# A hybrid decoder layer on one core: expert sums kept in PSUM, a ring of 24 weight slots, and a finer last transfer

## The chip, the core and the metric

The kernel runs on one core of a Trainium2 chip. The metric is the device time of one execution, in microseconds. TensorE is called PE below, VectorE DVE, ScalarE ACT, GpSimd POOL and SyncE SP. A transfer is a DMA that SP or ACT issues into its own queue.

## The reference, cut to what matters

The input is 256 tokens of 1024 float32 channels. A first part (norm, a combined projection, three mixers, merge gates, an output projection) adds to the residual `h`. A second part is a mixture of 32 experts in 4 groups; each token takes the best group and its two best experts there. The reference computes every expert for every token and weighs the results:

```
xn = rms_norm(h, norm2_g)
for e in range(32):
    hid = silu(xn @ w1[e]) * (xn @ w3[e])          # 1024 -> 256
    out = out + combine[:, e:e + 1] * (hid @ w2[e])  # 256 -> 1024
h = h + out
return rms_norm(h, final_norm_g)
```

The weights of the experts are 96 MiB in float32, and each is read once.

## The kernel before, in words

**The ring.** Nearly all weights pass through `ring`, a buffer of `SLOTS` = 22 slots, each of 2048 floats on 128 partitions (1 MiB). In the first part of the kernel the slots hold that part's weights, their high and low halves and scratch; each slot is given to an expert chunk by `early(...)` (L514) as soon as its last other use is over. Small buffers such as `qT`, `att`, `con`, `hidg` and `hidu` lie beside the ring.

**Expert chunks.** Four experts (`EB`) make a block, there are 8 blocks, and a block has 12 chunks: chunks 0 to 7 are the eight 128-row pieces of `w1` and `w3`, chunks 8 to 11 are `w2` by quarters of 256 output columns. Two rounds of four blocks (`ROUND` = 4) make one pass, and the inputs need one pass. So 96 chunks are loaded: 22 of them early, 74 while the experts are computed.

**Which slot a chunk takes.** `AT` gives the slot of each of the 48 chunks of a round: `[0..21, 0..17, 4..7, 18..21]`. SP issues the chunks in order. Ahead of each it waits until `expert_used` says that the chunk that held the slot (`earlier(c)`) was used: first six single chunks (L582), then pairs of 2 MiB (L585), the round's last two singly (L588), and for the second round the same in a loop (L596, L600). The queue is in order, so a chunk that waits for its slot holds back all behind it. By `AT`, the chunks 40 to 43 of the first round go into slots 4 to 7, which chunks 26 to 29 held, 14 chunks before.

**A block on PE.** For each of the 8 first chunks, four matmuls (one for each expert, on 32 rows of 128x32 stationary data) add into `bank[0]` (L1759). Between them `gather` (L1727) collects the tokens of the block, with the one-hot matrix `sel`, out of `xn2`, the normed and scaled copy of `h`. Banks 2 and 3 take its halves, ACT copies the one (L895) and DVE the other (L1315) to `xgT`. ACT applies Silu (L900), DVE multiplies (L1323), PE turns the result (L1782), ACT copies it (L902). Then come the four column quarters: `second(qt)` (L1794) multiplies by `w2` into bank 4 or 5, ACT copies the quarter to `yN` (L907), and `combine(qt)` (L1804) spreads it to the tokens by `cmbT`, into banks 6 and 7. DVE adds each result to `h` in SBUF (L1329); PE waits for that (`add_done`) before it writes the bank again. In a block `second(qt + 1)` stands before `combine(qt)`, and the last combine stands alone.

**Before and behind the experts.** POOL multiplies `h` by `norm2_g` into `xn2` (L661), ACT scales that by the token's reciprocal root (L883). PE runs `keep_busy` (L1374) while DVE works out the routing. The gain of the final norm, `fing`, is loaded by ACT at the start of the experts. At the end, ACT squares `h` in three parts as they become final (L926), POOL takes the power -0.5 (L683), DVE and ACT scale one token tile each (L1364, L944), and four transfers of 256 KB write the output.

Of the kernel before, what the change touches and what calls it, by code (L numbers as in the profile page):

```python
# [34 lines left out]
NQT = D // QC  # L35
CAP = 32
# [5 lines left out]
SLOTS = 22  # L42
# [66 lines left out]
K_DIST = K_ID + P  # L109
K_CB = K_DIST + 3 * P  # L110
K_CM = K_CB + NT * HEADS * 16
K_IC = K_CM + NT * 16
K_TRI = K_IC + 2 * T
# [7 lines left out]
K_N = K_FOLD2 + RC  # L121

TAKEN = 1024.0


def build(nc, x, params, consts, front, projs, small, wgrp, vecs, routerw, routerb, experts, out):
    with ExitStack() as ctx:
# [10 lines left out]
        def sem(name):  # L138
# [6 lines left out]
        con = sb("con", [P, K_N])  # L145
# [11 lines left out]
        qT = sb("qT", [P, REP, T])  # L157
        kv = sb("kv", [P, 4 * T])
        gts = sb("gts", [P, NT, GATES])
        hidg = sb("hidg", [P, 4, 2 * NCMP])  # L160
        hidu = sb("hidu", [P, 4, 2 * NCMP])
# [5 lines left out]
        att = sb("att", [P, 6 * 3 * P])  # L167
        qcur = sb("qcur", [P, T])
        npass = sb("npass", [P, 1], I32)
# [21 lines left out]
        sPT = att[:, 12 * P:18 * P].rearrange("p (b k) -> p b k", b=2)  # L191
# [12 lines left out]
        osplit = over("osplit", [P, 2, 4, T], "att")  # L204
# [18 lines left out]
        qflat = qT[:].rearrange("p r t -> p (r t)")  # L223
        comb = qflat[:, 320:384].rearrange("p (t e) -> p t e", t=NT)
        mask = qflat[:, 384:448].rearrange("p (t e) -> p t e", t=NT)
        rank = qflat[:, 448:512].rearrange("p (t e) -> p t e", t=NT)

        xn2 = att[:, 0:NT * D].rearrange("p (t d) -> p t d", t=NT)
        fin = xn2
# [9 lines left out]
        lg, gap1, key1, first, left, gap2, key2, second_of, both = [  # L239
            qflat[:, 448 + NT * NE // 2 + 32 + i * NT * RC:448 + NT * NE // 2 + 32 + (i + 1) * NT * RC] if i < 6 else  # L240
            qflat[:, (i - 6) * NT * RC:(i - 5) * NT * RC] for i in range(9)]
# [7 lines left out]

        g2b = con[:, K_DIST:K_DIST + D]  # L250
        fing = con[:, K_DIST:K_DIST + D]

        ident = con[:, K_ID:K_ID + P]
        dist = con[:, K_DIST:K_DIST + 3 * P]
# [4 lines left out]
        cmask = con[:, K_CM:K_CM + NT * 16].rearrange("p (t c) -> p t c", c=16)  # L259
        icnt = con[:, K_IC:K_IC + 2 * T].rearrange("p (a t) -> p a t", a=2)  # L260
        rk8 = con[:, K_RK:K_RK + PER_GROUP]
        fold = con[:, K_FOLD:K_FOLD + 32]
        fold2 = con[:, K_FOLD2:K_N]
# [13 lines left out]
        expert_in = [sem(f"expert_in{i}") for i in range(SLOTS // 2)]  # L277
        last_in = sem("last_in")
# [79 lines left out]
        xn2_done = sem("xn2_done")  # L358
        h2T_full = sem("h2T_full")
        h2T_done = [sem(f"h2T_done{i}") for i in range(2)]  # L360
        gained2 = sem("gained2")
# [19 lines left out]
        gained_most = sem("gained_most")  # L381
# [7 lines left out]
        add_done = sem("add_done")  # L389
# [77 lines left out]
        def second_out(qt, rows):  # L467

            return bank[4 + qt % 2][rows, 0:QC]

        def combined(t):

            return bank[6 + t][:, 0:QC]
# [4 lines left out]
        def _(sp):  # L478
# [42 lines left out]
            sp.dma_start(con[:, P:], consts[:, P:]).then_inc(con_in, 16)  # L521
# [38 lines left out]
            front_chunk(CH_NSA, 1)  # L560
            front_chunk(CH_WO, 0)
# [4 lines left out]
            front_chunk(CH_WO + 1, 1)  # L566

# [10 lines left out]
            early(SLOT_XHI, SLOTS)  # L578

            for c in range(SLOTS, SLOTS + SINGLES):  # L580
                sp.wait_ge(expert_used, earlier(c) + 1)
                sp.dma_start(ring[:, AT[c]], single(c)).then_inc(expert_in[AT[c] // 2] if c % 2 else single_in, 16)  # L582
            for c in range(SLOTS + SINGLES, NC - 2, 2):
                sp.wait_ge(expert_used, earlier(c + 1) + 1)
                sp.dma_start(slots_of(c), experts[c // NQ, c % NQ // 2]).then_inc(expert_in[AT[c] // 2], 16)  # L585
            for c, sem_in in ((NC - 2, expert_in[AT[NC - 2] // 2]), (NC - 1, last_in)):
                sp.wait_ge(expert_used, earlier(c) + 1)
# [1347 lines left out]
```

## Time and profile before

| | |
|---|---|
| median of 3 runs | 422.76 us (422.14 to 422.81) |
| the profiled execution's own time | 422.27 us |
| its span, first to last instruction | 420.4 us |
| outside the span | 1.87 us |
| mean granted PE clock | 0.985 |
| PE, DVE, ACT busy in the span | 388.5, 201.9, 141.7 us |
| bytes moved by transfers | 140.29 MB, mean 334 GB/s |
| first expert matmul | 219.42 us after the span's start |

Times in the rows are from the start of the span. The time beside the span is launch and end work that the trace doesn't show.

### The profile page before, as it was taken

What the parts mean: (1) busy time and instruction counts of PE and PEld (TensorE: products, weight loads), DVE (VectorE), ACT (ScalarE), POOL (GpSimd) and SP (SyncE); (2) the same over time, 40 slices, a digit from 0 to 9 for tenths busy, and PEclk for the clock granted to TensorE, in tenths of its full rate; (3) what the DMA queues carried; (4) which work ended last, traced back from release to release, by engine and by line L of the source; (5) the groups of instructions that cost most, each with busy time, mean ns of one, the idle gap of its engine ahead of it and who ended that gap; (6) DMA issues with size and microseconds to landing.
All of it is one profiled execution on the core that took longest, in us unless ns stands there. A gap on an engine that the chain in (4) does not pass through costs nothing.

```text
span 420.4 us, 7086 instructions
## 1 busy us (share of the span) xinstructions
PE 388.5 (92%) x2802; PEld 259.2 (62%) x2802; DVE 201.9 (48%) x392; ACT 141.7 (34%) x257; POOL 18.9 (4%) x39
## 2 busy tenths in 40 slices
PE   7999999999999999999989999999999778779682
PEld 5998988677777777888764545454435324234241
DVE  3838683999898595683362323231222203103113
ACT  6734352638565535242340303030302003011014
POOL 3000000300000000000520000000000000000002
PEclk9999999999999999999999999999999989979998
DMA  8999999634352495578999999899999999999972
GB/s 308 419 409 341 405 380 372 225 142 143 119 191 74 152 372 175 197 282 330 416 400 331 431 426 426 330 432 424 427 429 426 424 432 426 432 427 427 426 321 100
DMA packets 16871, 140.29 MB, mean 334 GB/s; under 512 B 2128, under 2 KB 2512, under 8 KB 5072
## 3 DMA queue, kind: packets, MB, share of 16 engines
q1 hardware_dynamic: 15696, 138.07, 81.9%
q10 hardware_dynamic: 1152, 1.88, 1.3%
q8 instruction: 17, 0.28, 0.3%
q14 instruction: 6, 0.05, 0.0%
HBM read 138.90 MB, written 1.05 MB: 333 GB/s over the span
## 4 chain that ended last, share of the span: by engine, by line
PE 69%; DMA 21%; DVE 6%; issue 1%; ACT 1%; POOL 0%; SPq 0%; POOLq 0%; DVEq 0%; PEldq 0%
DMA ring<-in_experts 20%; PE bank L1759 10%; PE bank L1794 5%; PE bank L1531 5%; PE bank L1727 5%; PE bank L1804 4%; PE bank L1532 4%; PE bank L1533 4%; PE bank L1389 4%; PE bank L1391 4%; PE bank L1390 4%; PE bank L1652 2%; PE bank L1654 2%; PE bank L1653 2%; PE bank L1493 1%; PE bank L1519 1%
## 5 line engine op out<-in xcount | busy, mean ns | idle before, releaser
L1759 PE MATMUL bank<-ring,kv 128*32 128x512 f32 x512 | 67.6, 632 | 13.4 <-DMA ring<-in_experts 13.3
L461 DVE TENSOR_TENSOR part<-ring,part 128x2048 fp32r<-128x2048 f32 (+1 forms) x26 | 57.8, 2231 | 16.9 <-ACT part L454 16.9
L454 ACT CAST part<-ring 128x2048 fp32r<-128x2048 f32 (+1 forms) x26 | 48.0, 1847 | 30.5 <-DMA ring<-in_front 30.3
L1329 DVE TENSOR_TENSOR h<-h,bank 128x256 f32<-128x256 f32 x64 | 26.9, 421 | 60.2 <-PE bank L1804 59.8
L1727 PEld LDWEIGHTS bank<-qcur,att 128*128 128x128 f32 x256 | 31.7, 191 | 28.2 <-issue 28.2
L1531 PE MATMUL bank<-part,xhi 128*128 128x512 f32 x96 | 39.2, 408 | 0.0
L1727 PE MATMUL bank<-qcur,att 128*128 128x128 f32 x256 | 39.1, 289 | 0.0
L1794 PE MATMUL bank<-ring,hidT 128*32 128x256 f32 x512 | 33.8, 385 | 4.8 <-DMA ring<-in_experts 4.2
L900 ACT ACTIVATE cw<-bank 128x256 f32<-128x256 f32 x8 | 3.1, 383 | 103.8 <-PE bank L1759 103.8
L1532 PE MATMUL bank<-part,xhi 128*128 128x512 f32 x96 | 37.5, 391 | 0.0
L1533 PE MATMUL bank<-part,xlo 128*128 128x512 f32 x96 | 37.5, 391 | 0.0
L1759 PEld LDWEIGHTS bank<-ring,kv 128*32 128x32 f32 x512 | 12.8, 111 | 39.9 <-issue 25.6
L1389 PE MATMUL bank<-xhi,part 128*128 128x256 f32 x128 | 36.6, 286 | 0.5 <-DVE xlo L977 0.5
L1804 PE MATMUL bank<-gab,vbd 128*128 128x256 f32 x128 | 36.2, 405 | 0.7
L1390 PE MATMUL bank<-xlo,part 128*128 128x256 f32 x128 | 36.2, 283 | 0.0
L1391 PE MATMUL bank<-xhi,part 128*128 128x256 f32 x128 | 36.2, 283 | 0.0
L1804 PEld LDWEIGHTS bank<-gab,vbd 128*128 128x128 f32 x128 | 21.0, 188 | 16.1 <-DVE h L1329 9.2
L907 ACT COPY gab<-bank 128x256 f32<-128x256 f32 x32 | 11.9, 371 | 47.4 <-PE bank L1794 47.4
L1323 DVE TENSOR_TENSOR vbd<-cw,bank 128x256 f32<-128x256 f32 x8 | 3.4, 421 | 50.2 <-ACT cw L900 50.2
L1389 PEld LDWEIGHTS bank<-xhi,part 128*128 128x128 f32 x128 | 24.5, 192 | 1.7 <-DVE xlo L977 0.9
L1794 PEld LDWEIGHTS bank<-ring,hidT 128*32 128x32 f32 x512 | 13.8, 109 | 18.2 <-issue 5.3
L1390 PEld LDWEIGHTS bank<-xlo,part 128*128 128x128 f32 x128 | 24.6, 192 | 0.0
(250 smaller groups left out, 548.8 us busy)
## 6 DMA issues: line engine op xcount, KB each, us to landing
ring<-in_experts SPq DMA_DIRECT2D x32, 2048.0 KB, 29.9
ring<-in_experts SPq DMA_DIRECT2D x32, 1024.0 KB, 8.6
ring<-in_front SPq DMA_DIRECT2D x28, 1024.0 KB, 5.9
ring<-in_front SPq DMA_DIRECT2D x4, 512.0 KB, 6.8
ring<-in_projs SPq DMA_DIRECT2D x4, 512.0 KB, 5.1
ring<-in_front SPq DMA_DIRECT2D x2, 560.0 KB, 9.2
h<-in_x SPq DMA_DIRECT2D x2, 512.0 KB, 3.9
con<-in_vecs ACTq DMA_DIRECT2D x2, 512.0 KB, 7.8
```

The lines of the kernel that those rows point to most:

```text
L454: nc.scalar.copy(high(n, half)[:, 0:c].bitcast(F32R), raw(n, half)[:, 0:c]).then_inc(hi_done, 1)
L461: nc.vector.tensor_tensor(low(n, half)[:, 0:c].bitcast(F32R), raw(n, half)[:, 0:c], high(n, half)[:, 0:c], ALU.subtract).then_inc(split_do ...
L1389: mm(dst, whi, ahi, start=start, stop=False)
L1390: mm(dst, whi, alo, start=False, stop=False)
L1391: return mm(dst, wlo, ahi, start=False, stop=stop)
L1531: mm(bank[t][:], XH[:, kk, cols], whi[:, k], start=(kk == 0), stop=False)
L1532: mm(bank[t][:], XH[:, kk, cols], wlo[:, k], start=False, stop=False)
L1533: ins = mm(bank[t][:], XL[:, kk, cols], whi[:, k], start=False, stop=(kk == KT - 1))
L1727: ins = mm(bank[2 + k // 4][:, (k % 4) * P:(k % 4 + 1) * P], xn2[:, t, k * P:(k + 1) * P], flat(sel[:, t]), start=(t == 0), stop=(t == NT ...
L1759: ins = mm(bank[0][CAP * e:CAP * (e + 1)], xgT[:, q, CAP * e:CAP * (e + 1)], expert(j, q, e), start=(q == 0), stop=(q == NQ1 - 1))
L1794: ins = mm(second_out(qt, slice(CAP * e, CAP * (e + 1))), hT[:, ht, CAP * e:CAP * (e + 1)], second_weights(j, qt, ht, e), start=(ht == 0), ...
L1804: mm(combined(t), cmbT[:, t * P:(t + 1) * P], yN[:, qt * QC:(qt + 1) * QC], start=True, stop=True).then_inc(comb_done, 1)
```

## The change

It has six parts. **Ring:** `SLOTS` is 24 and `AT` is `[0..23, 0..23]`, so that each chunk waits for the one 24 before it. The room comes from `att` and `qT` (with the half of `con` that only the first part reads, now `conf`), which move into slots 22 and 23, from the second copy `xn2`, which is no more, and from `hidg` and `hidu`, now laid over `qcur`. SP loads slot 23 early once `pc_done` is set, and slot 22 after the last NSA projection (`y_full`). **Sums:** before the experts, PE copies `h` into banks 4 to 7 by a matmul with the identity, in place of `keep_busy`. Each combine adds into these banks (`start=False`), the DVE adds and `add_done` are gone, and the squares and final scalings read the banks. `second` uses banks 0 and 3, gather bank 2 alone. **Norm:** gather reads `h` itself. `norm2_g` is applied when `xgT` is copied: four ACT activations of 128x128 in place of one copy of 128x512, and a DVE product in place of its copy. The token's reciprocal root is carried to the slots by two matmuls with one column and is the scale of Silu and of the DVE product. POOL's and ACT's passes over `xn2` are gone. **Pieces:** the columns are combined in five pieces, the last quarter as two of 128. In a round's last block the order is 0, 1, combine 0, combine 1, 2, combine 2, 3, 4, combine 3, combine 4. **Transfers:** a round's last chunk is issued as two halves with a semaphore each; `norm2_g`'s broadcast load is gone, and `fing` is loaded by SP behind the last chunk, into a slot that has become free. **Loop:** PE's code for the last round stands behind the loop as a copy of its own.

```
-SLOTS = 22
+SLOTS = 24
-AT = [*range(SLOTS), *range(18), *range(4, 8), *range(18, SLOTS)]
+AT = [*range(SLOTS), *range(SLOTS)]
+PIECES = ((0, 256), (256, 512), (512, 768), (768, 896), (896, 1024))
...
+            sp.wait_ge(scT_full, 1)
+            sp.wait_ge(pc_done, 1)
+            early(SLOT_Q, SLOTS)
             front_chunk(CH_WO, 0)
...
             front_chunk(CH_WO + 1, 1)
+            sp.wait_ge(y_full, 2 * N_G)
+            early(SLOT_ATT, SLOT_Q)
...
-            for c, sem_in in ((NC - 2, expert_in[AT[NC - 2] // 2]), (NC - 1, last_in)):
+            for c, f, sem_in in ((NC - 2, slice(0, ECHUNK), expert_in[AT[NC - 2] // 2]), (NC - 1, slice(0, half), last_half_in),
+                                 (NC - 1, slice(half, ECHUNK), last_in)):
...
+            sp.wait_ge(expert_used, passes * (NC * NB // ROUND) + (GIVEN - NQ + 2))
+            sp.dma_start(fing[:], vecs.to_broadcast([P, D])).then_inc(vec_in, 16)
...
-                    nc.gpsimd.tensor_tensor(xn2[:, t, c], h[:, t, c], g2b[:, c], ALU.mult).then_inc(gained2, 1)
...
-                nc.scalar.copy(flat(xgT[:, 0:4]), bank[2][:]).then_inc(xg0_done, 1)
+                for k in range(4):
+                    ins = nc.scalar.activation(xgT[:, k], bank[2][:, k * P:(k + 1) * P], ACT.Copy, scale=prm[:, PR_G2 + k:PR_G2 + k + 1])
+                ins.then_inc(xg0_done, 1)
...
-                nc.vector.tensor_tensor(hN, sl1, bank[0][:, HID:2 * HID], ALU.mult).then_inc(hn_done, 1)
-                for qt in range(NQT):
-                    for t in range(NT):
-                        dve.wait_ge(comb_done, b * (NT * NQT) + (NT * qt + t + 1))
-                        hv = h[:, t, qt * QC:(qt + 1) * QC]
-                        nc.vector.tensor_tensor(hv, hv, combined(t), ALU.add).then_inc(add_done, 1)
+                nc.vector.scalar_tensor_tensor(hN, bank[0][:, HID:2 * HID], rslot, sl1, ALU.mult, ALU.mult).then_inc(hn_done, 1)
...
             hidden(blocks)
             second_copy(blocks, 0)
             second_copy(blocks, 1)
-            second_copy(blocks, 2)
             last_square(0, 0)
             last_square(0, 1)
+            second_copy(blocks, 2)
+            last_square(1, 0)
+            last_square(1, 1)
             second_copy(blocks, 3)
-            for n in (1, 2):
-                for t in range(NT):
-                    last_square(n, t)
+            second_copy(blocks, 4)
+            last_square(2, 0)
+            last_square(2, 1)
...
-            keep_busy(8, ident, con[:, K_TRI:K_TRI + 2 * P])
+            for t in range(NT):
+                mm(bank[4 + t][:], ident, h[:, t, 0:512], start=True, stop=False)
+            for qt in (2, 3):
+                for t in range(NT):
+                    mm(summed(t, qt), ident, h[:, t, qt * QC:(qt + 1) * QC], start=(t == 0), stop=False)
...
+                            for t in range(NT):
+                                ins = mm(bank[1][:, T:T + 1], flat(sel[:, t]), stat[:, 26 + t:27 + t], start=(t == 0), stop=(t == NT - 1))
...
-                            pe.wait_ge(add_done, b * (NT * NQT) + (NT * qt + t + 4))
-                            mm(combined(t), cmbT[:, t * P:(t + 1) * P], yN[:, qt * QC:(qt + 1) * QC],
-                               start=True, stop=True).then_inc(comb_done, 1)
+                            ins = mm(sum_of_piece(t, p), cmbT[:, t * P:(t + 1) * P], yN[:, columns(p)],
+                                     start=False, stop=last and j == ROUND - 1 and (p == 1 or p in (2, NP - 1) and t == NT - 1))
+                        ins.then_inc(comb_done, 1)
```

## Rows read from the trace of the kernel before

**Rows 1.** The page: costliest groups, busy and mean, then idle before and its releaser.

```profile
L1759 PE MATMUL bank<-ring,kv 128*32 128x512 f32 x512 | 67.6, 632 | 13.4 <-DMA ring<-in_experts 13.3
L1329 DVE TENSOR_TENSOR h<-h,bank 128x256 f32<-128x256 f32 x64 | 26.9, 421 | 60.2 <-PE bank L1804 59.8
```

**Rows 2.** Windows of whole blocks: length, busy by engine, PEclk, DMA share, GB/s.

```profile
219.40:240.40 21.00, 20.88 (x180) 10.29 (x180) 5.98 (x14) 5.26 (x9) 0.00 (x0) 1.00 0.95 371
282.40:305.00 22.60, 21.65 (x181) 10.18 (x180) 5.71 (x14) 4.04 (x9) 0.00 (x0) 1.00 1.01 428
385.40:413.00 27.60, 22.01 (x181) 10.30 (x180) 5.92 (x15) 4.40 (x14) 1.91 (x2) 1.00 0.80 340
```

**Rows 3.** Windows of the expert stage on either side of the gap at 267 us.

```profile
232.00:266.00 34.00, 33.82 (x295) 17.09 (x288) 9.34 (x22) 7.27 (x14) 0.00 (x0) 1.00 1.01 427
272.00:404.00 132.00, 113.42 (x915) 52.84 (x914) 28.85 (x67) 18.90 (x40) 0.00 (x0) 0.96 1.01 427
```

**Rows 4.** The page's DMA issues: count, KB each, us from issue to landing.

```profile
ring<-in_experts SPq DMA_DIRECT2D x32, 2048.0 KB, 29.9
```

**Rows 5.** Line L600, the two last chunks: first and last start, then time to landing.

```profile
L600 SPq DMA_DIRECT2D ring<-in_experts x2: 333/548/764, 369.5 to 370.1; - x2
...
DMA to landing us min/median/max: 37.5/38.5/39.4
```

**Rows 6.** Windows of 1 us inside the gap.

```profile
267.00:268.00 1.00, 1.00 (x13) 0.36 (x16) 0.80 (x3) 0.00 (x0) 0.00 (x0) 1.00 0.31 131
268.00:269.00 1.00, 1.00 (x14) 0.26 (x8) 0.38 (x1) 0.00 (x0) 0.00 (x0) 1.00 0.12 49
269.00:270.00 1.00, 1.00 (x16) 0.29 (x12) 0.00 (x0) 0.00 (x0) 0.00 (x0) 1.00 1.49 279
270.00:271.00 1.00, 1.00 (x16) 0.23 (x8) 0.00 (x0) 0.00 (x0) 0.00 (x0) 1.00 0.73 295
```

**Rows 7.** Timeline of SP's queue: start, length, line, count.

```profile
184.16 0.33 SPq L495 DMA_DIRECT2D ring<-in_front  x1
...
189.86 1.28 SPq L514 DMA_DIRECT2D ring<-in_experts  x3
...
220.54 7.58 SPq L582 DMA_DIRECT2D ring<-in_experts  x6
...
268.07 2.53 SPq L585 DMA_DIRECT2D ring<-in_experts  x3
```

**Rows 8.** Windows where the two new early loads would fall.

```profile
159.00:162.00 3.00, 3.00 (x17) 2.52 (x16) 0.67 (x1) 2.29 (x2) 0.00 (x0) 1.00 0.69 208
...
189.00:192.00 3.00, 3.00 (x19) 2.58 (x18) 1.11 (x1) 2.83 (x3) 0.00 (x0) 1.00 0.37 76
```

**Rows 9.** Timeline of PE in a block: one second product, one combine.

```profile
252.37 1.07 PE L1794 MATMUL bank<-ring,hidT 128*32 128x256 f32 x16
...
255.01 1.13 PE L1804 MATMUL bank<-gab,vbd 128*128 128x256 f32 x4
```

**Rows 10.** Timeline of the end: PE's last products, ACT's squares.

```profile
404.70 1.93 PE L1794 MATMUL bank<-ring,hidT 128*32 128x256 f32 x32 [0.85 <-DMA ring<-in_experts]
...
409.82 0.63 ACT L926 ACTIVATE kv<-h 128x512 f32<-128x512 f32 x1 [0.68 <-DVE h L1329]
...
410.69 2.34 PE L1804 MATMUL bank<-gab,vbd 128*128 128x256 f32 x8
...
413.10 0.42 ACT L926 ACTIVATE otmp<-h 128x256 f32<-128x256 f32 x1 [0.27 <-DVE h L1329]
```

**Rows 11.** ACT: a plain first copy (timeline), an activation with a scale column (by form).

```profile
218.53 0.37 ACT L910 COPY kv<-bank 128x256 f32<-128x256 f32 x1 [2.62 <-PE bank L1736]
...
L712 ACT ACTIVATE xhi<-bank,prm 128x256 fp32r<-128x256 f32 x8 | 3.3, 492 | 0.1
```

**Rows 12.** Windows and timeline of PE behind long waits for chunks.

```profile
336.00:339.00 3.00, 2.95 (x16) 0.69 (x16) 0.00 (x0) 0.00 (x0) 0.00 (x0) 0.50 0.98 415
...
370.28 3.40 PE L1759 MATMUL bank<-ring,kv 128*32 128x512 f32 x16 [2.10 <-DMA ring<-in_experts]
```

More of the change, by code:

```diff
@@ L221, in build @@
         mlo = over("mlo", [P, KT, T], "ring", SLOT_XLO * SLOT)
[L223 to L229, printed above, removed]
+        routed = over("routed", [P, 3, NT, NE], "wg")
+        comb, mask, rank = routed[:, 0], routed[:, 1], routed[:, 2]
+        fin = over("fin", [P, NT, D], "ring", 12 * SLOT)
+        fing = over("fing", [P, D], "ring", 13 * SLOT)
+        last_squares = over("last_squares", [P, NT, D], "ring", 14 * SLOT)
         xgT = kv[:].rearrange("p (k s) -> p k s", k=KT)
@@ L237, in build @@
         lgT = qcur[:]
-        lg, gap1, key1, first, left, gap2, key2, second_of, both = [
-            qflat[:, 448 + NT * NE // 2 + 32 + i * NT * RC:448 + NT * NE // 2 + 32 + (i + 1) * NT * RC] if i < 6 else
-            qflat[:, (i - 6) * NT * RC:(i - 5) * NT * RC] for i in range(9)]
+        lg, gap1, key1, left, gap2, key2 = [kv[:, i * NT * RC:(i + 1) * NT * RC] for i in range(6)]
+        first, second_of, both = [yN[:, i * NT * RC:(i + 1) * NT * RC] for i in range(3)]
         top1, big1, top2, big2, behind, e2, weight, c1, c2, total = [vflat[:, 256 + 16 * i:256 + 16 * i + NT * ROWS] for i in range(10)]
@@ L465, in xT, with columns, second_out, summed @@
             return bank[(0, 1, 2, 3, 6, 7, 5, 5)[k]][:, (k == 7) * T:((k == 7) + 1) * T]
[L467 to L473, printed above, removed]
+        def columns(p):
+            return slice(*PIECES[p])
+        def second_out(p, rows):
+            return bank[(0, 3)[p % 2]][rows, 0:PIECES[p][1] - PIECES[p][0]]
+        def summed(t, qt):
+            c = t * QC if qt > 1 else qt * QC
+            return bank[4 + t if qt < 2 else 4 + qt][:, c:c + QC]
+        def sum_of_piece(t, p):
+            c0, c1 = PIECES[p]
+            return summed(t, c0 // QC)[:, c0 % QC:c0 % QC + c1 - c0]
         block = ctx.enter_context(nc.Block())
@@ L879, in _ @@
             nc.scalar.copy(lgT, bank[0][:, 0:T]).then_inc(lgT_done, 1)
-            act.wait_ge(gained2, 2 * NT)
-            act.wait_ge(rstd_done, NT + 1)
-            for t in range(NT):
-                nc.scalar.activation(xn2[:, t], xn2[:, t], ACT.Copy, scale=stat[:, 26 + t:27 + t]).then_inc(xn2_done, 1)
-            act.wait_ge(xn2_done, NT)
-            act.dma_start(fing, vecs[1:2].to_broadcast([P, D])).then_inc(vec_in, 16)
             act.wait_ge(sub_done, 1)
@@ L914, in _ @@
                 hidden(b + 1)
-                for qt in range(NQT):
-                    second_copy(b + 1, qt)
+                for p in range(NP):
+                    second_copy(b + 1, p)
                 gathered_copy(b + 1)
@@ L1742, in _, with round_of_blocks @@
             passes = pe.value_load(npass[0:1, 0:1], min_val=1, max_val=MAXPASS)
-            with pe.Fori(0, passes * (NB // ROUND)) as bb:
+            def round_of_blocks(bb, last):
                 for j in range(ROUND):
@@ L1809, in _ @@
                         gather(3)
-                    for qt in range(1, NQT):
-                        second(qt)
-                        combine(qt - 1)
-                    combine(NQT - 1)
+                    second(1)
+                    combine(0)
+                    if j < ROUND - 1:
+                        second(2)
+                        combine(1)
+                        second(3)
+                        combine(2)
+                    else:
+                        combine(1)
+                        second(2)
+                        combine(2)
+                        second(3)
+                    second(4)
+                    combine(3)
+                    combine(4)
+            with pe.Fori(0, passes * (NB // ROUND) - 1) as bb:
+                round_of_blocks(bb, False)
+            round_of_blocks(pe.value_load(npass[0:1, 1:2], min_val=1, max_val=MAXPASS * (NB // ROUND) - 1), True)
 def constants():
```

206 lines of the change are left out of this document (107 added, 99 removed).

## Prediction

> **What bounds the kernel now.** I began at the page's costliest groups [rows 1]. PE is busy nearly all the time, but its largest idle time, 13.3 us, stands before the first expert product and waits for expert chunks. The DVE adds into `h` are short, and DVE waits long before them, so DVE bounds nothing. Next, the windows by block [rows 2]: a block lasts 21.0 us while PE sets the pace (22.6 for a round's last block, where no later gather fills the waits), and 27.6 us in the last, with 22.0 busy. Then the windows of the transfers [rows 3]: 427 GB/s from 232 to 266 us and again from 272 to 404. A block's 12 chunks are 12.58 MB, so 29.5 us at that rate. PE needs 21. The expert stage is therefore a race that starts with a full ring and that the transfers lose: their last landing sets the end. The time from issue to landing, 29.9 us for the pairs [rows 4], says the same: SP issues far ahead. The last two chunks, issued at 369.5 and 370.1 us, landed after 37.5 and 39.4 us: 407.0 and 409.5 [rows 5]. So a chunk takes 2.5 us, by the rate 1.0486 MB / 427 GB/s = 2.46 us. The end is 420.4, which is 10.9 us behind the last landing. The sum has three terms: how many chunks are left when the race starts, where the transfers pause, and the 10.9 us.
>
> **Two chunks fewer in the race.** The stream begins when chunk 0 is used: first issue at 220.54 [rows 7]. With 24 slots 72 chunks are left, not 74: 2 x 2.46 = -4.9 us, if the two others find idle transfer time earlier. Slot 23 is issued once `pc_done` is set, near 159 us, where transfers move 208 GB/s, a share of 0.69 [rows 8]; the queue's next member waits for PE's gate products anyway. Slot 22 is issued when the last NSA product is done, the event that releases the front transfer at 184.16; the next issue is at 189.86 [rows 7], and 189 to 192 us moves 76 GB/s [rows 8]. Each needs 2.5 us and has some 5. If neither fitted, the term would be 0: its other bound.
>
> **The pause goes.** The windows from 267 to 271 us move 131, 49, 279 and 295 GB/s [rows 6]: 296 + 378 + 148 + 132 = 954 KB short of 427, or 2.2 us. SP issues again at 268.07 [rows 7]. By `AT`, chunk 40 takes slot 4, which chunk 26 held; it is in block 2, which begins at 219.4 + 2 x 21.0 = 261.4, so its use is near 267. SP's order holds back all behind. After the change chunk 40 waits for chunk 16, used some 20 us earlier. For any chunk the distance is 24, PE needs 1.75 us for a chunk and the transfers 2.46, so once started they wait for no slot: -2.2 us. Bounds: 0, if the pause has another cause, and -2.2. The last half then lands at 409.5 - 4.9 - 2.2 = 402.4.
>
> **The start of the race.** PE's gather, and so block 0, hardly moves. The first copy of 128x256 took 0.37 us at 218.53 and block 0 began at 219.42, 0.5 us later than the copy allowed [rows 11]. Two activations of 128x128 with a scale column replace it. An activation with a scale of 128x256 took 0.49, a plain copy 0.37 [rows 11]; for 128 columns I bound one by 0.25 and 0.4, so the two by 0.5 and 0.8: both inside the 0.37 + 0.5 us there is. The identity products replace `keep_busy` product for product in columns (2 x 512 + 4 x 256 for 8 x 256) in the wait for DVE's routing; hidden. One more small DVE step lies beside the gather. I take 0. POOL's and ACT's passes over `xn2` were not what PE waited for, so dropping them gains 0. The early broadcast of `fing`, 0.52 MB, leaves a stretch of full transfers: at most -1.2 us, taken as 0 since the next issue waits for chunk 0.
>
> **PE's work per block, and its cover.** Gone: the wait for a DVE add in a lone combine, between nothing and one add (0.42 us [rows 1]); the two last combines take 2.34 us where one takes 1.13 [rows 9, 10], so I take 0.1. Added: two products with one column, bounded by 0 and by the 0.28 us that each of a combine's four records takes, 1.1 us; I take 0.3. ACT's four activations (1.0 to 1.6 us) replace a copy near 0.6 us, between the last piece's copy and the next block: after the last `second`, ACT needs 0.35 + 1.0 to 1.6 us, PE's two half combines 1.1; a wait of 0.3 to 0.9, say 0.6. In a round's last block the combines wait for their copies, some 1 us more. Together +0.7 us a block, 1.0 to 2.0 at the bounds. The cover is PE's lead over the chunks: alone, it would reach the last block's second products at 219.4 + 7 x 21.0 + 1.6 + 14 = 382; the chunks admit it at 404.6 now, 397.5 after. That is 15.5 us for 8 blocks, 1.9 us a block. So this costs 0; beyond 1.9 us each block would pay the excess.
>
> **Behind the last landing.** A second product of 256 columns takes 1.0 us, a combine 1.1 [rows 9]; pieces of 128, half; an ACT copy 0.37, or 0.26 for 128; a pair of squares of 512 columns 1.3 (0.63 each, start to start 0.63 [rows 10]), of 256 0.95, each with its read of the sum. Count from the last landing, X. The pair with quarters 0 and 1 lands at X - 4.9, as now [rows 10]. Second 0 and 1 to X - 2.9, combine 0 and 1 to X - 0.8, second 2 to X + 0.2. ACT now squares ahead of copy 2: to X + 0.6, the copy to X + 1.0, combine 2 to X + 2.1. Pieces 3 and 4: to X + 3.2, while ACT squares part two to X + 3.1, copies 3 and 4 to X + 3.7. Combine 3 and 4: to X + 4.6. Before it was 413.03 [rows 10], X + 3.5. So the split pieces do not shorten the end here: +1.1 us. The halves give piece 3 its weights 1.2 us sooner, but PE is not there yet. Behind the combine come squares, means, power, scaling, output: 7.4 us, the same but for DVE's final scaling in three instructions in place of two, +0.1. Bounds of this part: 0 (ACT and PE overlap better than I count) and +2.5 (every activation at its upper bound, and a wait for each piece).
>
> `fing` is issued behind the last half. By the queue's order it lands some 1.2 us later, X + 1.3 to 3; DVE needs it for two products that must end by X + 5.6, so until X + 4.3 it costs nothing.
>
> The Trainium skill (DMA: Bandwidth & Descriptors, Measured) has a single 1 MB transfer at 341 GB/s and says that smaller ones are worse, which speaks against the halves. In a full queue 1 MB follows the one before in 2.5 us [rows 5], so the trace does not agree for queued transfers; by the page's fixed part of 2.0 us (Anatomy of one DMA) for one more transfer, the estimate would be 2 us later than the sum below.
>
> **The sum.** -4.9 - 2.2 + 1.1 + 0.1 = -5.9 us. The profiled span of 420.4 becomes 414.5, its time 416.4. The profiled time lies 0.5 below the median, from which the sum gives 416.9; I say 416.6. This case alone spans 415.2 to 418.0.
>
> **Rivals.** (a) The pause stays, because something else stops SP near 268: 416.6 + 2.2 = 418.8. Against it: the place fits `AT` to a microsecond. (b) The early loads push front weights or find no room: up to 4.9 lost, 421.5. Against: the windows above. (c) Less happens behind the landing or the freed 0.52 MB counts: 416.6 - 1.1 - 1.2 = 414.3. (d) The other side: PE's clock falls in the last block. After waits of 2.5 and 2.1 us for chunks the granted clock was 0.50 of full, the 1.2 GHz level, in one stretch from 336 us, and at 370 us 16 expert products took 3.40 us [rows 12], where 16 take 67.6 / 512 x 16 = 2.1 on the mean [rows 1]. In the last block now the same kind of wait left the clock at 1.00 [rows 2], perhaps as gathers lie between. If it falls there in part, +1 to +3: 417.6 to 419.6. If it falls from the last waits through to the last combine, some 11 us of PE work, half of the block's 22.0 [rows 2], grow by 0.6 of themselves (3.40 over 2.1) to 1.0 (the two levels); by 0.75 it is +8, 424.6; slower than now from +7.0 on. The Trainium skill (TensorE: Matmul & The Clock Gate, HAM oscillation) says that an engine whose work between waits is shorter than the waits falls back every time; by that rule this rival holds. The trace agrees near 336 and 370 us [rows 12], and not in the last block [rows 2]. (e) PE becomes the bound: at 2.0 to 2.8 us more a block it gives back up to all, 417 to 423; needs more than my upper bounds.
>
> **Chances.** The sum 0.62; (c) 0.08; (a) 0.08; (b) 0.06, spread 417 to 423; (d) in part 0.09, in full 0.04; (e) 0.03. Two runs of this kernel can be told apart from about 0.2%, 0.85 us: faster is under 421.9, slower over 423.6. Slower: (d) in full and a little of (e), 0.05. Same: the far ends of (b), (d) and (e), 0.04. Faster 0.91. The range 414.8 to 419.0 takes in (a), most of (c) and (d) in part.
>
> **What would show it.** Right: issues in the first round without a gap near 268; transfers at 427 GB/s from 232 us until the last landing near 402.4; PE's first long wait later, near 355 us in place of 333; last combine 4 to 5 us behind the landing; end at 414.5. Wrong: a window under 300 GB/s after 232 us; `fing` landing later than 4 us behind the last half; a granted clock of 0.5 after 392 us; blocks longer than 23 us before 340 us.

## The result, and the profile after

The changed kernel takes 416.78 us (median of 4 runs, 416.37 to 418.11) against 422.57 of the kernel before on the same chip (4 runs, 422.14 to 422.81): a ratio of 0.987, with an interval of 0.9852 to 0.9888. The gain, 1.4%, is small but clear of the noise. The profiled execution, the fastest of the four, took 416.37 us with a span of 414.6. The forecast was 416.6 and 414.5. That the total fits says little yet, for it is a sum of terms that could have missed in opposite directions, so each is read by itself.

The page of the changed kernel: the costliest group (busy and mean, then idle before and its releaser) and the issues of the pairs (count, KB, us to landing).

```profile
L1781 PE MATMUL bank<-ring,kv 128*32 128x512 f32 x512 | 64.1, 607 | 6.9 <-DMA ring<-in_experts 3.9
...
ring<-in_experts SPq DMA_DIRECT2D x31, 2048.0 KB, 30.9
```

PE's waits for chunks ahead of the expert products fell from 13.3 us [rows 1] to 3.9, yet the end moved by 5.8. So PE's idle time is not what the end follows. SP's queue shows the transfers (start, length, line, count):

```profile
153.00 6.26 SPq L509 DMA_DIRECT2D ring<-in_front  x2
159.38 0.36 SPq L528 DMA_DIRECT2D ring<-in_experts  x1
...
184.53 24.05 SPq L528 DMA_DIRECT2D ring<-in_experts  x12
220.54 7.92 SPq L602 DMA_DIRECT2D ring<-in_experts  x6
...
259.80 3.33 SPq L610 DMA_DIRECT2D ring<-in_experts  x3
266.87 87.10 SPq L618 DMA_DIRECT2D ring<-in_experts  x23
354.22 12.64 SPq L624 DMA_DIRECT2D ring<-in_experts  x3
382.71 0.34 SPq L627 DMA_DIRECT2D fing<-in_vecs  x1
```

The first early load stands at 159.38, the second is the first of the twelve from 184.53. The first transfer that waits for chunk 0's use is issued at 220.54, the same time as before to 0.01 us [rows 7]. The last three expert issues and `fing`, by their lines (time to landing):

```profile
L624 SPq DMA_DIRECT2D ring<-in_experts x3: 4035/4070/4107, 354.2 to 362.8; - x3
...
DMA to landing us min/median/max: 40.6/43.5/46.6
...
L627 SPq DMA_DIRECT2D fing<-in_vecs x1: 339/339/339, 382.7 to 382.7; - x1
...
DMA to landing us min/median/max: 21.9/21.9/21.9
```

The queue lands them in order: 354.2 + 46.6 = 400.8, the last half 362.8 + 40.6 = 403.4, `fing` 382.7 + 21.9 = 404.6. The forecast had 402.4 for the last half. Windows of the changed kernel (length, busy by engine, PEclk, DMA share, GB/s):

```profile
162.00:165.00 3.00, 3.00 (x15) 2.17 (x15) 1.66 (x1) 1.85 (x2) 0.00 (x0) 1.00 1.03 429
189.00:192.00 3.00, 3.00 (x19) 2.57 (x18) 1.07 (x1) 2.87 (x3) 0.00 (x0) 1.00 0.93 350
220.00:232.00 12.00, 11.87 (x104) 5.94 (x100) 2.48 (x7) 2.13 (x3) 0.00 (x0) 1.00 0.86 315
232.00:266.00 34.00, 33.14 (x330) 18.33 (x328) 2.42 (x6) 7.52 (x21) 0.00 (x0) 1.00 1.01 429
266.00:272.00 6.00, 6.00 (x58) 2.70 (x54) 1.94 (x5) 1.28 (x1) 0.00 (x0) 1.00 1.01 431
272.00:398.00 126.00, 115.27 (x1058) 60.76 (x1050) 12.78 (x32) 23.43 (x61) 0.00 (x0) 0.99 1.01 425
219.40:241.40 22.00, 21.53 (x206) 11.61 (x207) 3.04 (x8) 4.82 (x12) 0.00 (x0) 1.00 0.91 357
285.40:309.50 24.10, 21.89 (x204) 11.60 (x204) 2.42 (x6) 4.83 (x12) 0.00 (x0) 1.00 1.01 428
389.00:391.00 2.00, 2.00 (x16) 1.09 (x12) 0.00 (x0) 0.00 (x0) 0.00 (x0) 0.69 0.96 410
391.00:393.00 2.00, 2.00 (x9) 0.34 (x3) 0.00 (x0) 0.00 (x0) 0.00 (x0) 0.50 1.00 426
```

The gap near 268 us [rows 6] is gone: 431 GB/s. The idle place at 189 us [rows 8] now moves 350 GB/s where it moved 76. The load issued at 159.38 moves a little later than the window that was looked at [rows 8]: 159 to 162 us is as it was, at 210 GB/s, and 162 to 165 moves 429 where it moved 147, 165 to 168 moves 295 where it moved 232. A block takes 22.0 us where it took 21.0, a round's last block 24.1 where it took 22.6 [rows 2]. And the clock fell to the 1.2 GHz level, 0.50, for a stretch in the last block, near 391 to 393 us. The end of the changed kernel, as a timeline (start, length, engine, line, operation, count, idle before):

```profile
398.48 1.93 PE L1821 MATMUL bank<-ring,hidT 128*32 128x256 f32 x32 [0.63 <-DMA ring<-in_experts]
400.34 1.99 PE L1831 MATMUL bank<-gab,vbd 128*128 128x256 f32 x8
402.26 1.07 PE L1821 MATMUL bank<-ring,hidT 128*32 128x256 f32 x16
402.37 0.60 ACT L931 ACTIVATE last_squares<-bank 128x512 f32<-128x512 f32 x1 [1.53 <-PE bank L1831]
...
403.53 0.37 ACT L911 COPY gab<-bank 128x256 f32<-128x256 f32 x1
404.04 1.10 PE L1831 MATMUL bank<-gab,vbd 128*128 128x256 f32 x4 [0.71 <-ACT gab L911]
...
405.08 1.08 PE L1821 MATMUL bank<-ring,hidT 128*32 128x128 f32 x32
...
405.91 0.58 ACT L911 COPY gab<-bank 128x128 f32<-128x128 f32 x2
406.23 1.16 PE L1831 MATMUL bank<-gab,vbd 128*128 128x128 f32 x8
...
407.43 0.38 ACT L931 ACTIVATE last_squares<-bank 128x256 f32<-128x256 f32 x1 [0.94 <-PE bank L1831]
```

The last combine ends at 407.39, 4.0 us behind the last landing, where it was 3.5 [rows 10]. From there to the end of the span are 7.2 us, before 420.4 - 413.03 = 7.4. So the sum as measured: two chunks -4.9, pause -2.2, +1.0 for a stream that lands later than these two alone would give, +0.5 for the combine, -0.2 behind it: -5.8 us, and 420.4 - 5.8 = 414.6. The last three are read; the split of the first two is what the experiments have to show.

One thing more is in the trace. In the semaphore events each transfer's landing is a count of 16 parts, and the transfer has landed with the last. Of the last transfer of the weights, the first and the last part came at 407.42 and 409.53 us before, and at 399.80 and 403.33 us in the changed kernel: the parts lie 3.5 us apart where they lay 2.1. For the transfers that land from 279 to 338 us the distance is 2.1 us as before; from the one at 344 us on it is 3.3, and then up to 3.6. A window at the end shows the same: the DMA share is down to 0.37 while the last half is still awaited.

```profile
402.00:403.00 1.00, 1.00 (x18) 0.42 (x16) 0.00 (x0) 0.63 (x3) 0.00 (x0) 1.00 0.37 147
```

Between the transfers at 338 and 344 us, at 340.9, stands a packet of 16 KB in the queue that loads the engines' instructions; it took 1.1 us, where most of the weights' packets of that size took 0.61. From 310 to 400 us the changed kernel has six such packets, and the kernel before has none:

```profile
q8 instruction: 6, 0.10, 0.4%
```

### The profile page after: what moved, and what is told of

Its sections match the earlier page's. It is cut to its first block, busy times and chain, and to the rows that moved or that the text cites. A ratio compares the mean times of both kernels' runs of the same rounds, so it can differ in the third digit from the quotient of the medians.

```text
span 414.6 us, 7327 instructions
## 1 busy us (share of the span) xinstructions
PE 388.9 (94%) x2990; PEld 269.0 (65%) x2990; DVE 176.9 (43%) x340; ACT 145.4 (35%) x285; POOL 12.8 (3%) x33
## 4 chain that ended last, share of the span: by engine, by line
PE 47%; issue 46%; DVE 5%; POOL 1%; ACT 0%; POOLq 0%; DVEq 0%
PE bank L1545 5%; PE bank L1547 4%; PE bank L1546 4%; PE bank L1403 4%; PE bank L1404 4%; PE bank L1405 4%; PE bank L1668 2%; PE bank L1666 2%; PE bank L1667 2%; PE bank L1507 1%; PE bank L1533 1%; PE bank L1519 1%; PE bank L1388 1%; PE bank L1565 1%; PE bank L1465 1%
## 5 line engine op out<-in xcount | busy, mean ns | idle before, releaser
L1781 PE MATMUL bank<-ring,kv 128*32 128x512 f32 x512 | 64.1, 607 | 6.9 <-DMA ring<-in_experts 3.9
L1321 DVE TENSOR_TENSOR kv<-bank,prm 128x512 f32<-128x512 f32 x8 | 5.5, 692 | 109.4 <-PE bank L1749 109.4
L1749 PEld LDWEIGHTS bank<-qcur,h 128*128 128x128 f32 x256 | 32.3, 194 | 28.4 <-issue 28.4
L1749 PE MATMUL bank<-qcur,h 128*128 128x128 f32 x256 | 39.8, 293 | 0.0
L1821 PE MATMUL bank<-ring,hidT 128*32 128x256 f32 (+1 forms) x640 | 35.2, 342 | 3.2 <-DMA ring<-in_experts 2.7
L1831 PE MATMUL bank<-gab,vbd 128*128 128x256 f32 (+1 forms) x160 | 36.3, 359 | 1.4 <-ACT gab L911 1.3
L1546 PE MATMUL bank<-part,xhi 128*128 128x512 f32 x96 | 37.5, 390 | 0.0
L1831 PEld LDWEIGHTS bank<-gab,vbd 128*128 128x128 f32 x160 | 24.6, 189 | 12.2 <-issue 10.3
L911 ACT COPY gab<-bank 128x256 f32<-128x256 f32 (+1 forms) x40 | 13.2, 330 | 51.0 <-PE bank L1821 50.9
L1821 PEld LDWEIGHTS bank<-ring,hidT 128*32 128x32 f32 x640 | 16.6, 109 | 17.1 <-issue 8.1
L1403 PEld LDWEIGHTS bank<-xhi,part 128*128 128x128 f32 x128 | 24.5, 192 | 1.9 <-DVE xlo L982 1.1
L1405 PEld LDWEIGHTS bank<-xhi,part 128*128 128x128 f32 x128 | 24.6, 192 | 0.0
```

The source lines that it names most:

```text
L1403: mm(dst, whi, ahi, start=start, stop=False)
L1405: return mm(dst, wlo, ahi, start=False, stop=stop)
L1546: mm(bank[t][:], XH[:, kk, cols], wlo[:, k], start=False, stop=False)
L1749: ins = mm(bank[2][:, (k % 4) * P:(k % 4 + 1) * P], h[:, t, k * P:(k + 1) * P], flat(sel[:, t]), start=(t == 0), stop=(t == NT - 1))
L1781: ins = mm(bank[0][CAP * e:CAP * (e + 1)], xgT[:, q, CAP * e:CAP * (e + 1)], expert(j, q, e), start=(q == 0), stop=(q == NQ1 - 1))
L1821: ins = mm(second_out(p, slice(CAP * e, CAP * (e + 1))), hT[:, ht, CAP * e:CAP * (e + 1)], second_weights(j, p, ht, e), start=(ht == 0), s ...
```

## The experiments

Each ratio is to the kernel before, with its 95% interval. The changed kernel was run again beside them:

> The changed kernel as it is, on the chip of the next three, as their measure: 416.8.

Measured: 416.69 us (416.38 to 416.85), 0.9857 (0.9837 to 0.9876), span 414.5.

### The pause put back

```
-AT = [*range(SLOTS), *range(SLOTS)]
+AT = [*range(SLOTS), *range(16), *range(2, 6), *range(20, SLOTS)]
```

> The changed kernel with one thing put back: in the first round chunks 40 to 43 again take slots that chunks 26 to 29 held, 14 chunks before (24 slots stay, two chunks are still loaded early). Theory (the pause near 267 us came from the slot table): SP again holds the queue until chunk 27 is used. That use is now near 270.5 us, while the stream runs dry near 262.4, so the pause is longer than it was, some 8 to 10 us, and nothing later gives it back: 425 to 427 us. Rival (the pause had another cause, and the gain is the two early chunks and lighter blocks): no change, 416.8.

Measured: 426.51 us (426.38 to 426.82), 1.0092 (1.0078 to 1.0107). Windows of this kernel:

```profile
262.00:264.00 2.00, 1.59 (x16) 1.20 (x16) 0.00 (x0) 1.31 (x5) 0.00 (x0) 1.00 0.24 98
264.00:268.00 4.00, 4.00 (x36) 2.25 (x32) 0.07 (x1) 0.00 (x0) 0.00 (x0) 1.00 0.01 4
268.00:272.00 4.00, 4.00 (x38) 1.50 (x34) 1.86 (x5) 1.28 (x1) 0.00 (x0) 1.00 0.32 53
272.00:274.00 2.00, 2.00 (x21) 0.44 (x13) 0.00 (x0) 0.00 (x0) 0.00 (x0) 1.00 0.65 254
```

They fall short of 427 GB/s by 0.66 + 1.69 + 1.50 + 0.35 = 4.19 MB, or 9.8 us, and the second products that wait for the last pair start 10.0 us later than in the changed kernel:

```profile
408.49 1.93 PE L1821 MATMUL bank<-ring,hidT 128*32 128x256 f32 x32 [0.67 <-DMA ring<-in_experts]
```

Chunk 40 again takes the slot of chunk 26. Nothing but the table is altered, so the order of the slots alone makes the pause, and all of it reaches the end. It is 9.8 us and not 2.2; an estimate from the rows gives most of that: the two spare chunks bring the stream to chunk 40 some 4.9 us sooner, and PE, whose blocks are 1 us longer, comes to chunk 26 some 2 us later, 2.2 + 4.9 + 2 = 9.1. So with this table the rest of the change would have made the kernel slower. The table also has a shorter distance, 10 chunks, at the start of the second round (its chunk 2 takes the slot that chunk 40 held), and that one makes no second pause: 274 to 404 us moves 424 GB/s.

### The two early loads put back into the race

```
-            sp.wait_ge(scT_full, 1)
-            sp.wait_ge(pc_done, 1)
-            early(SLOT_Q, SLOTS)
...
-            sp.wait_ge(y_full, 2 * N_G)
-            early(SLOT_ATT, SLOT_Q)
...
+            sp.wait_ge(expert_used, GIVEN + 1)
+            early(SLOT_ATT, SLOTS)
             for c in range(SLOTS, SLOTS + SINGLES):
```

> The changed kernel with its two added early loads (slots 22 and 23) issued only when chunk 0 was used, ahead of the others. 74 chunks are then in the race again. Theory: the last landing is 2 x 2.46 us later, 416.8 + 4.9 = 421.7. Rival (the gain comes from the slot table and the sums in PSUM, not from where the two loads fall): 416.8 to 417.3.

Measured: 420.71 us (420.69 to 420.82), 0.9954 (0.9939 to 0.9968); span 418.8. One line of PE's timeline and one window of this kernel, 220 to 232 us:

```profile
402.71 1.93 PE L1818 MATMUL bank<-ring,hidT 128*32 128x256 f32 x32 [0.63 <-DMA ring<-in_experts]
```

```profile
220.00:232.00 12.00, 11.87 (x104) 5.84 (x98) 2.58 (x7) 2.13 (x3) 0.00 (x0) 1.00 0.87 345
```

The pair's second products start 4.2 us later than at 398.48, not 4.9. The window accounts for the rest: with three chunks asked for at once, this kernel moves 345 GB/s there and the changed kernel 315, which is 0.36 MB or 0.8 us at 427 GB/s. Two chunks fewer in the race are worth 4.2 here, 4.9 by count. The rival, no change, is out.

The other way to have them early, both asked for at the very end of the early loads, with the two earlier issues taken out:

```
             early(SLOT_XHI, SLOT_ATT)
+            early(SLOT_ATT, SLOTS)
```

> The changed kernel with the two added early loads issued last of all early loads, near 209 us, without waiting for chunk 0. They then move from 219 to about 223.7 us, into the time in which the stream would stand still (119 and 53 GB/s from 218 to 222). Theory (what counts is that 72 chunks are left and that the two lie in idle time, wherever that is): the first raced chunk starts about 1.2 us later, but it and the next find a full queue, which gives back some 0.7: 416.8 to 417.4. Rival (they must be loaded before the stretch of full transfers, or all of 4 to 5 us is lost as when they were issued at chunk 0's use): 420.7.

Measured: 417.09 us (417.0 to 417.27), 0.987 (0.9854 to 0.9887). The windows show the two chunks moving beside the last gather:

```profile
218.00:220.00 2.00, 1.69 (x16) 0.80 (x14) 0.85 (x2) 0.60 (x2) 0.20 (x1) 1.00 0.99 410
220.00:222.00 2.00, 2.00 (x20) 1.12 (x16) 0.00 (x0) 0.00 (x0) 0.00 (x0) 1.00 1.04 430
```

It starts the second products 0.7 us later than the changed kernel, at 399.15. So what counts is that the transfers were idle somewhere before the race; the hole from 218 to 222 us, where the changed kernel moves 119 and 53 GB/s, serves nearly as well as those at 162 and 189 us.

### How much more work PE could bear

After each `pe.wait_ge(hT_done, b + 2)` PE does one or four products more, into a part of a bank that nobody reads:

```
+                    for _ in range(1):
+                        mm(bank[1][:, T:2 * T], ident, h[:, 0, 0:T], start=True, stop=True)
```

> The changed kernel with one more product of 256 columns in every block, written where nobody reads, ahead of the block's second products: 0.53 us of PE time a block, 4.2 in all. Theory (PE's work has cover up to the 6.6 us that it still waits for chunks in the last blocks, 0.8 a block): no change, 416.6 to 417.3. Rival (PE, busy in 94% of the span, bounds): 4.2 us slower, 421.0.

Measured: 417.06 us (416.94 to 417.8), 0.987 (0.9849 to 0.9891), span 415.1. Half a microsecond more a block is some 4 us of PE's work in all, and the median moves by 0.4 us at most: PE is not the bound of the changed kernel.

> The same with four such products a block: 2.1 us a block, 17 in all. Theory: the cover of 6.6 us is used up and the rest is paid, 416.8 + 17 - 6.6 = 427. Rival: all is paid, 434. If the cover were the 1.9 us a block that the prediction gave to all additions, of which 1.0 is used: 17 - 7 = 10, the same 427.

With range(4):

Measured: 423.70 us (423.5 to 423.85, 10 runs), 1.0023 (1.0014 to 1.0032); span 421.7. The second products of its last pair:

```profile
405.66 1.93 PE L1823 MATMUL bank<-ring,hidT 128*32 128x256 f32 x32
```

and PE's expert products from 219 us on:

```profile
L1781 PE MATMUL bank<-ring,kv 128*32 128x512 f32 x512 | 62.8, 599 | 3.0 <-issue 2.4 <-ACT kv L897 0.6
```

No wait for a chunk is left: here PE sets the end. Its block grew from 22.0 to 23.9 us, 15.3 us in eight, and the second products moved by 405.66 - 398.48 = 7.2. The other 8.1 us were cover, 1.0 us a block. The expectation was 427 and missed by 3.3: it took the added work as 17 us, and the cover as the 6.6 us of waits that can be seen in the changed kernel (3.9 + 2.7). So the waits on show understate the cover by 1.5 us. Most of that is in the expert products, which are busy for 64.1 us in the changed kernel and 62.8 here, at a mean granted clock of 0.991 and 0.996 over the whole span.

### The pieces and the transfers at the end

The last chunk in one transfer, in both rounds, and one wait of PE for it:

```
-            for c, f, sem_in in (..., (NC - 1, slice(0, half), last_half_in),
-                                 (NC - 1, slice(half, ECHUNK), last_in)):
+            for c, f, sem_in in (..., (NC - 1, slice(0, ECHUNK), last_in)):
```

> The changed kernel with a round's last chunk in one transfer and one semaphore; the five pieces stay. Theory (PE comes to piece 3 only 1.7 us after the last landing): no change, 416.5 to 417.1. Rival one (the halves let PE start sooner): 1.2 us slower, 418.0. Rival two (small transfers cost more): 0.3 to 2 us faster.

Measured: 416.99 us (416.38 to 417.5), 0.986 (0.9846 to 0.9874): no change.

Besides that, the last quarter in one piece of 256 again:

```
-PIECES = ((0, 256), (256, 512), (512, 768), (768, 896), (896, 1024))
+PIECES = ((0, 256), (256, 512), (512, 768), (768, 1024))
```

> The changed kernel with four pieces of 256 columns, and so one last transfer; the sums stay in PSUM, and in a round's last block combine 2 stays ahead of second 3. Theory: PE's work behind the last landing is the same, one copy less waits: 416.5 to 417.3, blocks about 0.4 us shorter with no effect. Rival (the finer pieces shorten the tail): 417.9 or more.

Measured: 418.30 us (417.81 to 420.29, 6 runs), 0.9906 (0.9888 to 0.9923), where the rival, not the theory, had put it. In the profiled execution its last combine starts like this:

```profile
406.77 1.10 PE L1823 MATMUL bank<-gab,vbd 128*128 128x256 f32 x4 [0.58 <-ACT gab L908]
```

It ends at 407.87, 0.5 us later than in the changed kernel, while its last chunk landed at 403.3 as there; the span is 415.1. So the finer pieces do shorten the tail, which the theory denied. The spans of its six runs go from 415.1 to 417.1, and 2.0 to 3.2 us of the time lie outside them, where all other kernels here have 1.7 to 2.0. Of the two halves of this edit I can say that the split transfer is worth nothing by itself and that the split piece takes 0.5 us off the tail; the remaining 1 us stays unexplained.

The last part in another order. PE does the second product of piece 3 before combine 2, and ACT copies before it squares:

```
-                        combine(1)
-                        second(2)
-                        combine(2)
-                        second(3)
+                        combine(1)
+                        second(2)
+                        second(3)
+                        combine(2)
...
-            last_square(0, 0)
-            last_square(0, 1)
             second_copy(blocks, 2)
-            last_square(1, 0)
-            last_square(1, 1)
+            last_square(0, 0)
+            last_square(0, 1)
             second_copy(blocks, 3)
             second_copy(blocks, 4)
+            last_square(1, 0)
+            last_square(1, 1)
```

> The changed kernel with another order in a round's last block: PE issues second 3 ahead of combine 2, and ACT copies piece 2 ahead of its first squares, pieces 3 and 4 ahead of the second. Theory (behind the pair's landing the end is a chain of PE and ACT in which PE waits 0.7 us for the copy of piece 2): PE waits less and the end comes 0.5 to 0.8 us earlier, 416.1. Rival (the last landing sets the end): no change.

Measured: 416.05 us (415.87 to 416.93), 0.9845 (0.9827 to 0.9863), span 414.1. Its timeline:

```profile
402.42 1.51 PE L1821 MATMUL bank<-ring,hidT 128*32 128x256 f32 x32
404.07 1.10 PE L1831 MATMUL bank<-gab,vbd 128*128 128x256 f32 x4
405.10 0.65 PE L1821 MATMUL bank<-ring,hidT 128*32 128x128 f32 x16
405.68 1.23 PE L1831 MATMUL bank<-gab,vbd 128*128 128x128 f32 x8
```

PE's wait for the copy of piece 2 is filled, and the last combine ends at 406.91, 0.5 us earlier, though its second products began 0.15 later, at 398.63. Its median is the lowest of all, 0.6 us under the 416.69 beside it, as forecast, but its interval overlaps that of the changed kernel.

### The sums in PSUM alone, and the clock

The kernel before, with its DVE adds cut to 8 of 256 columns:

```
-                        hv = h[:, t, qt * QC:(qt + 1) * QC]
-                        nc.vector.tensor_tensor(hv, hv, combined(t), ALU.add).then_inc(add_done, 1)
+                        hv = h[:, t, qt * QC:qt * QC + 8]
+                        nc.vector.tensor_tensor(hv, hv, combined(t)[:, 0:8], ALU.add).then_inc(add_done, 1)
```

> The kernel before with DVE's 64 additions into h cut to 8 of 256 columns each (it leaves the other columns of the experts' sum out); all waits stay. Theory (DVE and its adds bound nothing, the chunks do; keeping sums in PSUM brings time only by the room it makes and the adds at the very end): blocks at most 0.4 us shorter without effect, the end 0.3 to 0.7 us sooner: 422.0. Rival (PE's waits for the adds, 9.2 us of idle weight loads, are part of the time): 3 us or more faster, under 419.7.

Measured: 421.74 us (421.04 to 422.34, 11 runs), 0.9977 (0.9967 to 0.9986); span 420.2. So the cut adds are worth 0.9 us (0.6 to 1.4 by the interval), and the rival's 3 us are out. In the profiled execution the last combine ends at 413.00, before 413.03, and 7.2 us follow it where 7.4 did: the race is as it was, and what the adds delay stands behind the last landing. PE's waits for the adds, and a narrow rest of each, stay in this kernel, so the whole of the adds was not taken out; nor was the price of the sums in PSUM tried by itself.

In the last block, products that nobody reads stand ahead of two of PE's waits for chunks:

```
+                        if last and j == ROUND - 1 and q in (4, 6):
+                            pe.wait_ge(cmb_done, b + 1)
+                            for _ in range(4 if q == 4 else 2):
+                                mm(bank[1][:, T:2 * T], ident, h[:, 0, 0:T], start=True, stop=True)
```

> The changed kernel with four products of 256 columns that nobody reads ahead of step 4 of the last block and two ahead of step 6, where PE waits for chunks and the granted clock then fell to 0.5 for some 3 us. Theory (the fall cost about 1.4 us of PE time, which the wait for the pair of quarters 0 and 1 still covered, save for some 0.1 us): the clock stays at 1.00, the median hardly moves, 416.4 to 416.8, the slowest runs come closer. Rival (the fall is in the time): 1 us or more faster, under 415.7.

Measured: 416.69 us (416.32 to 418.0), 0.9856 (0.9841 to 0.9871). Windows of this kernel, to be held against the two last ones of the changed kernel above:

```profile
389.00:391.00 2.00, 0.82 (x8) 0.16 (x8) 0.00 (x0) 0.00 (x0) 0.00 (x0) 1.00 1.02 434
391.00:393.00 2.00, 2.00 (x17) 0.87 (x14) 0.00 (x0) 0.00 (x0) 0.00 (x0) 1.00 0.98 418
```

The clock stays at 1.00 and the median does not move: the slower products were covered, since PE waited for the last pair behind them anyway. The spread was expected to become narrower, and it did not: the profiled execution, the slowest of the four, had its second products at 400.08, 1.6 us later than the changed kernel, at full clock. So this late run comes from the transfers and not from the clock. Its stream is hardly slower: the last transfer's first part came at 400.16, 0.4 us later than in the changed kernel, but its last part at 404.91, so that the 16 parts lie 4.8 us apart. That distance grew in two steps, from 1.9 to 3.3 us between the transfers at 270 and 276 us and from 3.4 to 4.8 between 384 and 390, with instruction packets at 272.7 and 383.9.

Both together, this edit and the order of the last part:

> Both the other order of pieces in the last block and the filled waits. Theory: 416.05 less 0 to 0.3: 415.9, the fastest so far.

Measured: 416.26 us (416.11 to 417.01), 0.9855 (0.984 to 0.987), span 414.2: 0.4 over the forecast, and no better than the order alone.

## Why the prediction was right

**Two chunks fewer, forecast -4.9.** They found their room from 162 to 168 and near 189 us, and the race began at the same 220.54. Taken back alone they cost 4.2 us at the second products and 3.9 in the median. The term holds; as that kernel fills its queue sooner, 4.2 against 4.9 by count is no error of the sum.

**The pause, -2.2.** Right in cause and place: the order put back brings a pause at 262 to 274 us. What the prediction did not see is that the parts hang together: with the other parts in and the old distance of 14 the pause is 9.8 us long.

**The start of the race, 0.** The first issue is at 220.54 in both. Right.

**PE's work per block, +0.7 us against a cover of 1.9.** It was +1.0, inside the bounds, and +1.5 in a round's last block: 24.1 us, over the 23 that the prediction named as a sign against it. Of a cost at the end there is no sign. The cover is confirmed by the kernel with four products: 8.1 us were left, and 15.5 less 8 x 1.0 is 7.5. So that sign was too strict. Of the 1.0 us the products with one column (L1793) take 0.43, from 224.86 to the next start at 225.29, where 0.3 was forecast, and a wait before the next block's first products takes 0.32, where 0.6 was forecast; the rest is not read:

```profile
224.86 0.50 PE L1793 MATMUL bank<-stat,qcur 128*128 128x1 f32 x4
225.29 0.64 PE L1781 MATMUL bank<-ring,kv 128*32 128x512 f32 x4
...
241.39 1.07 PE L1781 MATMUL bank<-ring,kv 128*32 128x512 f32 x8 [0.32 <-issue]
```

**The last half at 402.4.** It landed at 403.3 to 403.4, the step that was mis-sized, by 1.0 us. The landings by parts split this. On the mean of its 16 parts the last transfer came 6.7 us earlier than before, not 7.1, and its last part 6.2, since the parts lie further apart. So some 0.4 us are a slower stream: 126 us at 425 in place of 427 GB/s are 0.6 us, and the stretch from 232 to 272 us gives 0.2 back. (From 220 to 232 us there is no real loss: 315 against 327 GB/s contains the end of the early `fing` load before, issued at 213.3 and landed at 221.9, and from 222 to 232 us it is 367 against 366.) And 0.5 us are the wider distance of the parts. Both fit the instruction packets, six of them after 310 us where there were none, and the part of the change that gives PE a second copy of its code is the likely source. The prediction has no term for it. That is argued from times that coincide; no run here puts the last round back into the loop.

**Behind the last landing, +1.1 and +0.1.** The path was as told: PE had just ended quarter 2 when the last half landed, and waited 0.71 us for the copy behind ACT's squares. But the last combine ended 4.0 and not 4.6 us behind the landing: against it, combines 0 and 1 were done some 0.3 us earlier than counted, and ACT's copy of piece 2 some 0.2 more. And what follows took 0.2 less instead of 0.1 more. The activations of the squares are shorter when they read PSUM, 0.60 and 0.38 us, before 0.63 and 0.42 [rows 10]; but the kernel before with narrow adds, whose squares read SBUF, has the same 7.2 us, so the missing adds may be the cause as well. The term was 0.3 in place of 1.2, which pays for the late landing: two errors of 0.9 and 1.0 us cancelled. That the total fits to 0.2 us is luck. The reading that the split pieces do not shorten the end was wrong in part: without them the last combine ends 0.5 us later. `fing` landed 1.2 us behind the last half, early enough.

The Trainium skill (DMA: Bandwidth & Descriptors, Anatomy of one DMA) has a fixed part of 2.0 us for a transfer, and has it for those that GpSimd issues. These are issued by SP: the two halves landed 1.3 us apart, at 402.1 and 403.3, and the kernel with one transfer in their place took 416.99 against 416.69 us, so no run here shows such a part for transfers that stand in a full queue.

**The rivals.** (a) is excluded by 431 GB/s at 266 to 272 us, (b) by the windows at 162 and 189 us and by the kernel in which the two loads do enter the race, 420.7. (c) is true in part, 0.9 us less behind the landing, with the landing against it; the freed 0.52 MB gave nothing, for 218 to 222 us moves only 119 and 53 GB/s. (d), the clock, came as far as its cause, and with it the prediction's sign against itself, a clock of 0.5 after 392 us: after a wait of 2.22 us for a chunk, the longest of the changed kernel's expert products, the clock was granted at 0.50 from 391 to 393 us, and 8 products took 1.94 us where 8 had taken 1.06:

```profile
388.69 1.06 PE L1781 MATMUL bank<-ring,kv 128*32 128x512 f32 x8 [2.22 <-DMA ring<-in_experts]
...
390.80 1.94 PE L1781 MATMUL bank<-ring,kv 128*32 128x512 f32 x8
```

It was back before the second products and cost nothing, because the last pair landed later anyway; filled waits kept the clock, without any time gained. The Trainium skill (TensorE: Matmul & The Clock Gate, HAM oscillation) says that an engine whose work between its waits is shorter than the waits falls back each time. The trace does not bear that out as the rule for this place: PE had worked for 7 us without a wait for a chunk before this one of 2.2 us, and the clock fell all the same. Nor do the rows of before fit its condition well: of the two waits ahead of 370 us, 2.6 and 2.1 us, the work between took 2.7. (e) needed 1.0 us a block more; with 1.9 more PE does become the bound, at 423.7.

The prediction's first long wait of PE near 355 us came near 362; blocks that are longer by 1.0 in place of 0.7 us put it later, as PE catches up with the chunks more slowly.

## What to carry to other kernels

Where transfers set the end, count the bytes that are left when the race starts and look for windows before it in which the queue is idle: a chunk moved there was worth most of its transfer time here (4.2 of 4.9 us for two), and 4 us of an engine's work within its cover 0.4 at most. In a ring, look for the shortest distance between a slot's use and its next fill while the stream still has spare slots: 14 made the pause in the first round, while 12 before the change and 10 in the kernel with the pause put back made none in the second. Slots added elsewhere made the short distance worse, 9.8 us for 2.2, since the stream comes to it earlier. One distance for all chunks has no such place. Measure the cover of an engine by adding work to it until the end moves, for the waits on show understated it, 6.6 for 8.1 us. And where the last landing sets the end, look at when its parts arrive, not only at the rate of the stream.

## What the runs showed of the hardware

Two transfers of 0.52 MB in a full queue land 1.3 us apart, at the same rate as whole chunks. The changed kernel's last three issues took SP 4.0 to 4.1 us each, with 40.6 to 46.6 us to the landing; the last two before the change took 0.3 and 0.8 us, with 37.5 and 39.4 [rows 5]. A transfer's 16 parts land 2.1 to 4.8 us apart in a full stream, and the steps in which this distance grew fall beside 16 KB packets of instructions that took 1.1 us. A square of 128x512 that reads PSUM takes 0.60 us and from SBUF 0.63, one of 128x256 takes 0.38 and 0.42. Nearly the same wait of PE for a chunk (2.1 to 2.6 us) lowers the clock in one block and not in another: before the change near 336 and 370 us and not in the last block [rows 2, 12], after it in the last; and there the kernel with four pieces waited 2.12 us and kept 1.00. What decides this stays open, as do the unexplained time of the kernel with four pieces and what brings an instruction packet into the stream at one moment or another.
